# Attention score products of two neighbouring jobs on two row groups of TensorE, on unpadded keys

## The reference, cut to what matters

```
# second block: 8 heads, head size 64, two branches (slc, win) over 2 key groups, and 8 moba heads
s = q @ k.T * scale - slope * dist        # dist is huge where the key is masked
p = softmax(s);  out += gate * (p @ v)    # (moba: out = p @ v)
# third block, twice: 4 heads each of na, dil (head size 64), mla (96), diff (two halves of 32)
s = q @ k.T * scale + bias
p = softmax(s);  out = p @ v              # diff: out = (p0 - lam * p1) @ v
```

## Time and profile before

| | |
|---|---|
| median of 3 runs | 2133.78 us (2132.88 to 2137.18) |
| span of the profiled execution | 2125.6 us; no time of its own is listed for it, and the median of the runs stands 8.2 us above the span |
| busy share of the span | PE 80%, PE weight loads 58%, DVE 38%, ACT 30%, POOL 4% |
| woven attention stages | second block 1267 to 1389 us; third block 1490 to 1571 us and 1825 to 1907 us |
| granted clock in them | 1.00 of full speed, 0.83 and 0.90 in the last 15 us of each layer of the third block |

### The profile page before, as it was taken

The page is one execution under the profiler, slowest core; times in us unless marked ns, Lnnn a source line. Parts: engine busy times, 40 slices in busy tenths (PEclk is TensorE's granted clock), DMA queues, the critical chain, the costliest instruction groups (busy, mean ns, idle before and its releaser), DMA issues.

```text
span 2125.6 us, 32653 instructions
## 1 busy us (share of the span) xinstructions
PE 1698.7 (80%) x13430; PEld 1230.6 (58%) x13430; DVE 808.9 (38%) x1592; ACT 646.7 (30%) x1144; POOL 84.0 (4%) x143
## 2 busy tenths in 40 slices
PE   5999975656665665666665799988999999999998
PEld 3889921211111221111111599988989988989996
DVE  2374621001101111100111457775656654666654
ACT  3334310000000000000000347654754434655433
POOL 2000010000000000000000200101100001000000
PEclk9999988877878778777778799999999999999999
DMA  9986789999999999999999853408065545146650
GB/s 367 334 317 230 287 366 428 429 429 427 429 429 429 429 429 429 427 429 428 429 429 429 321 199 120 140 18 285 21 197 165 195 170 179 53 139 189 198 179 20
DMA packets 152994, 613.49 MB, mean 289 GB/s; under 512 B 8816, under 2 KB 62138, under 8 KB 128312
## 3 DMA queue, kind: packets, MB, share of 16 engines
q1 hardware_dynamic: 148928, 604.47, 72.4%
q0 software_dynamic: 3200, 7.14, 1.2%
q10 hardware_dynamic: 760, 0.39, 0.1%
HBM read 610.88 MB, written 5.03 MB: 290 GB/s over the span
## 4 chain that ended last, share of the span: by engine, by line
PE 54%; DMA 38%; DVE 3%; ACT 1%; issue 1%; SPq 1%; DVEq 1%; POOL 0%; POOLq 0%; ACTq 0%
PE psum L1473 52%; DMA ring<-in_w_down_e 19%; DMA ring<-in_w_up_e 18%; DMA ring<-in_w_in 1%; PE psum L1843 1%; DVE ring_r L704 1%; SPq L750 0%; ACT arena L1070 0%; ACT ring_r L695 0%; PE psum L1578 0%; SPq L769 0%; DVE arena L2448 0%; POOL stat L945 0%; PE psum L2007 0%; PE psum L1992 0%
## 5 line engine op out<-in xcount | busy, mean ns | idle before, releaser
L1473 PE MATMUL psum<-ring,arena 128*32 128x512 f32 (+2 forms) x4314 | 537.6, 643 | 279.9 <-DMA ring<-in_w_up_e 128.1
L1473 PE MATMUL psum<-xR_r,ring_r 128*128 128x256 f32 x4416 | 542.9, 281 | 2.1 <-DVE xR_r L2087 1.3
L1473 PEld LDWEIGHTS psum<-xR_r,ring_r 128*128 128x128 f32 x4416 | 521.0, 188 | 12.7 <-issue 10.8
L1473 PEld LDWEIGHTS psum<-ring,arena 128*32 128x32 f32 x4314 | 155.3, 134 | 629.8 <-issue 211.9
L704 DVE TENSOR_TENSOR ring_r<-ring,ring_r 128x1024 fp32r<-128x1024 f32 (+2 forms) x332 | 377.9, 1172 | 192.0 <-ACT ring_r L695 191.3
L695 ACT CAST ring_r<-ring 128x1024 fp32r<-128x1024 f32 (+2 forms) x332 | 320.3, 1007 | 382.1 <-PE psum L1473 377.9
L1473 PE MATMUL psum<-arena 128*128 128x256 f32 (+7 forms) x1270 | 188.0, 374 | 21.2 <-DVE arena L2323 9.9
L2320 DVE TENSOR_TENSOR arena<-arena,psum 128x512 f32<-128x512 f32 x16 | 16.9, 1055 | 476.8 <-PE psum L1473 476.8
L1473 PE MATMUL psum<-ring_r,xR_r 128*128 128x256 f32 (+3 forms) x1344 | 170.8, 284 | 10.5 <-DVE xR_r L2072 6.9
L1473 PE MATMUL psum<-ring_r,arena_r 128*128 128x512 f32 (+1 forms) x912 | 168.2, 346 | 2.1 <-DVE mt L2699 2.1
L1473 PEld LDWEIGHTS psum<-ring_r,xR_r 128*128 128x128 f32 x1344 | 160.6, 191 | 13.2 <-DVE ring_r L704 7.2
(11 more groups left out here) (270 smaller groups left out, 959.6 us busy)
## 6 DMA issues: line engine op xcount, KB each, us to landing
ring<-in_w_gate_e SPq DMA_DIRECT2D x64, 2048.0 KB, 25.9
ring<-in_w_down_e SPq DMA_DIRECT2D x63, 2048.0 KB, 26.4
ring<-in_w_up_e SPq DMA_DIRECT2D x62, 2048.0 KB, 24.9
ring<-in_w_in SPq DMA_DIRECT2D x30, 2048.0 KB, 12.5
ring<-in_w_ada SPq DMA_DIRECT2D x12, 2048.0 KB, 13.8
ring<-in_w_gate SPq DMA_DIRECT2D x22, 1024.0 KB, 5.5
ring<-in_w_up SPq DMA_DIRECT2D x22, 1024.0 KB, 8.2
ring<-in_w_down SPq DMA_DIRECT2D x10, 2048.0 KB, 7.8
```

The costliest lines, as they stand in the source:

```text
L1473: return nc.tensor.matmul(o, l, r, start=s, stop=e)
```

## The change

The score products lose their padding and are issued in pairs. Jobs are ordered so that jobs n and n+1 (n even) are the two heads of one partition pair with the same t (slc, win, moba, na, dil), or the two halves of one diff head. At the even slot PE issues both score products, the first into bank 4 from its own rows, the second into bank 5 from its own rows; at the odd slot it issues none. Before the pair PE waits until DVE has read both scores of the pair before. DVE runs `least` for both jobs at the even slot and for none at the odd one; everything else stays in its slot. `jmin`, `jsum` and `jrec` get eight columns instead of four. The keys are stored once (`ksD`, `kwD`, `kbT`, `knT`, `kdT`), so ACT takes them in one copy, and POOL's clearing of the padded keys goes. mla jobs (96 rows) are issued in pairs too, on the rows they had. The core of the diff:

```diff
-JOBS3 = ([("na", h, 0, t) for h in range(4) for t in range(TT)]
+JOBS3 = ([("na", 2 * m + f, 0, t) for m in range(2) for t in range(TT) for f in range(2)]
...
-NSA_JOBS = [(br, h, t) for h in range(8) for br in ("slc", "win") for t in range(TT)]
-MOBA_JOBS = [("moba", h, t) for h in range(8) for t in range(TT)]
+NSA_JOBS = [(br, 2 * m + f, t) for m in range(4) for br in ("slc", "win") for t in range(TT) for f in range(2)]
+MOBA_JOBS = [("moba", 2 * m + f, t) for m in range(4) for t in range(TT) for f in range(2)]
...
+            rows_ = slice(HD * (h % 2), HD * (h % 2) + HD)
+            if kind == "diff":
+                rows_ = slice(HD * (h % 2) + 32 * c, HD * (h % 2) + 32 * c + 32)
+            kp = (kdT if kind == "diff" else knT)[rows_, h // 2, :]
...
-            return dict(q=qaT[:, h // 2, qs], k=kk[:, h % 2, g, 0:nk], widths=[P] * (t + 1), dist=dist,
+            kk, vv, i = (ksD, vs, 1) if br == "slc" else (kwD, vw, 2)
+            return dict(q=qaT[rows_, h // 2, qs], k=kk[rows_, g, 0:nk], widths=[P] * (t + 1), dist=dist,
...
-                pool.wait_ge(n3_xn, l * 3 + 2)
-                if l == 0:
-                    nc.gpsimd.memset(arena[:, 2 * D:3 * D], 0.0).then_inc(pad3_set, 1)
-                nc.gpsimd.memset(kdP.rearrange("p m f c t -> p (m f c t)"), 0.0).then_inc(pad3_set, 1)
...
-                        for lo, rows, d in KP[n]:
-                            o = nc.scalar.copy(d[lo:lo + rows], two(G(i)[lo:lo + rows, :]))
-                        o.then_inc(g3_free[i % 4], 1)
+                    elif n in KN:
+                        take(n, KN[n], src=two, l=l)
...
-            def scores(j, J, s_, m_, base=0):
+            def scores(j, pair_, s_, m_, base=0):
                 if j >= 2:
-                    pe.wait_ge(m_, base + (j - 1))
-                mm(psum[:, 4 + j % 2, 0:sum(J["widths"])], J["q"], J["k"]).then_inc(s_, 1)
+                    pe.wait_ge(m_, base + j)
+                for f, J in enumerate(pair_):
+                    mm(psum[:, 4 + f, 0:sum(J["widths"])], J["q"], J["k"]).then_inc(s_, 1)
...
-                        scores(n, job3(n, l), k_s, k_min, l * NJ3)
+                        if n % 2 == 0:
+                            scores(n, (job3(n, l), job3(n + 1, l)), k_s, k_min, l * NJ3)
...
-                    least(n, job2(n), j_s, j_t, j_min, t_need=n - 3 if n >= 4 else None)
+                    for j in ((n, n + 1) if n % 2 == 0 else ()):
+                        least(j, job2(j), j_s, j_t, j_min, t_need=j - 3 if j >= 4 else None)
```

More of the change, by code:

```diff
@@ L160 @@
 assert len(L3) % RING == 0
[L163 removed]
+JOBS3 = ([("na", 2 * m + f, 0, t) for m in range(2) for t in range(TT) for f in range(2)]
          + [("mla", h, 0, t) for h in range(4) for t in range(TT)]
          + [("diff", h, c, t) for h in range(4) for t in range(TT) for c in range(2)]
[L166 removed]
+         + [("dil", 2 * m + f, 0, t) for m in range(2) for t in range(TT) for f in range(2)])
 NJ3 = len(JOBS3)
@@ L1330, in _ @@
                 elif n[:2] == "kb":
-                    i = AT[n]
-                    piece(act, i)
-                    for f in range(2):
-                        o = nc.scalar.copy(kbP[HD * f:HD * f + HD, 2 * h:2 * h + 2, f, :], two(G(i)[HD * f:HD * f + HD, :]))
-                    o.then_inc(g_free[i % 4], 1)
+                    take(n, kbT[:, 2 * h:2 * h + 2, :], src=two)
                 elif n[:2] == "vb":
@@ L2607, in _ @@
                             biases(l)
-                        turned = l * NT3 + (TURN3[n - 4] + 1) if n - 4 in TURN3 else None
-                        least(n, job3(n, l), k_s, k_t, k_min, l * NJ3, sbuf3, turned)
+                        for j in ((n, n + 1) if n % 2 == 0 else ()):
+                            turned = l * NT3 + (TURN3[j - 4] + 1) if j - 4 in TURN3 else None
+                            least(j, job3(j, l), k_s, k_t, k_min, l * NJ3, sbuf3, turned)
                         if n >= 1 and PAIR3[n - 1]:
```

68 lines of the change are left out of this document (30 added, 38 removed).

## The result

The changed kernel takes 2148.78 us (median of 4 runs, 2147.16 to 2150.91) against 2134.41 us of the kernel before, measured beside it: ratio 1.0072, 95% interval 1.0056 to 1.0088 (the two medians by themselves give 1.0067). It is slower by 14.4 us; 10.8 were forecast, and the time lies inside the forecast's own range (2139 to 2151). A second comparison, with 6 runs of the changed kernel, gave 1.0081 (1.0065 to 1.0097).

What follows compares the result with a forecast made beforehand. PE was taken to bound the woven attention stages. Terms 0.3 + 7.2 + 5.3 - 2.0 = +10.8 us on a 2125.6 us span, with the median 8.2 above, gave 2144.6 us; forecast range 2139 to 2151, 8-in-10 range 2131 to 2154.

Steps and rivals of the forecast that it cites:

- second `least` ahead of `both` and `finish`: Woven stages: DVE's second `least` delays what PE waits for, 7.2 us at diff turns and 5.3 us for `finish`.
- PE's own work, +0.3: Woven attention stages: 44 pairs of 256 keys at -0.04 us and 12 of 128 at +0.17, sum +0.3 us.
- the rival that row groups enter and leave for nothing: Score pairs on PE: entry and exit cost nothing, giving 2131 us; chance 0.2 for nothing or nearly (2127 to 2136).
- Waits at diff turns, +7.2: Third block: PE waits 0.60 us for `both` at six diff turns in each of two layers, +7.2 us.
- Waits for `finish`, +5.3: Second block, t = 1 pairs: 8 waits of 0.47 us, 3 smaller for moba, two late 128-key places; +5.3 us.
- Key copies, -2.0: ACT's four key copies become one: -0.9 us a layer in the third block, -0.2 in the second; -2.0 us.
- Tail, 0: Last four jobs of each layer: the same work of values and `finish` is only reordered, 0 us.
- The median stands 8.2 above it: Whole kernel: 8.2 us added to the predicted span of 2136.4 to get the median, 2144.6 us.
- What the profile was to show: Stages grow some 5 us (second block) and 3 a layer, PE's busy time falls, waits for `both` and `finish` appear.

Runs made afterwards that it cites:

- `both` between: Changed kernel with `both` and `finish` moved between the two `least` at the even slot; 2135.47 us against 2132.91 of the kernel before, ratio 1.0014.
- order and storage alone: Kernel before with only the new job order and unpadded keys in one copy, no pairs or row groups, full rows; 2134.8 us against 2133.38, ratio 0.9999.
- the runs without pairs: Changed kernel with each score product on its row group and `least` in its own slot: 2169.85 us, ratio 1.0163 to before; same with full rows: 0.9999.
- Putting `least` back: Changed kernel with each job's `least` in its own slot again, score pairs kept; 2140.77 us against 2133.38 of the kernel before, ratio 1.0036.

## Why the prediction was right, by its own steps

Three of the kernels above split the change into its steps, since each differs from the next in one of them (us, all three stages to the last product of probabilities and values):

| step | forecast | the two kernels | difference |
|---|---|---|---|
| second `least` ahead of `both` and `finish` | +12.5 | changed, less `both` between | +12.3 |
| pairs on row groups | +0.3 | `both` between, less order and storage alone | +1.1 |
| order of jobs and key storage | -2.0 | order and storage alone, less before | +0.5 |
| sum | +10.8 | changed, less before | +13.9 |

The large step was priced rightly, place by place; the two small ones came out 0.8 and 2.5 us dearer. (Two profiles of one kernel differ by 0.1 and 0.3 us in this sum; a part of the first row may be the clock, see the tail below.) That the exponentials add up to just the forecast 10.8 is chance: they leave out 3 us at the ends of the layers.

**PE's own work, +0.3: right.** The way in, the two rounds, the way out and the exposed weights all have their forecast size in the rows above: 0.63 us for the pair, 1.10 with the values (forecast 1.11). The prediction priced entry and exit of row groups by column groups, for want of a row; the runs without pairs confirm the choice at 0.29 us a visit, and the rival that row groups enter and leave for nothing (2131 us) is refuted by the same runs. They were forecast to cost 0.29 each too, but of other parts: the second record's weights are exposed also in a single product (0.63 for two records), and behind it only 0.05 are (1290.88 to 1291.04, 0.16 instead of 0.11). With the way in, 0.09, that makes 0.34, of which 0.29 reached the stage; that the forecast's figure came out is in part luck. A pair of 128 keys takes 0.42 us to the next full record (1279.35 to 1279.77) where two full products take 0.44, so with the way in and the weights behind it the pair costs, as forecast.

**Waits at diff turns, +7.2: right in place and number, nearly in size.** Six a layer were forecast and six are there. At the pair shown the wait is 0.62 us by starts, 0.60 forecast. By the waits' view, which counts from the end of the last record, the twelve add up to 2.9 + 3.1 = 6.0 us. Putting `both` between the two `least` gave 6.6 us back in the two layers, to the last product.

**Waits for `finish`, +5.3: right.** Eight waits at slc and win pairs with t = 1 were forecast. There are seven for L2440, one of 0.75 us and six of 0.36 to 0.38, and an eighth place where ScalarE's copy of the turned tile came last (0.38): 3.3 us, 0.42 each, for 0.40 forecast. Moba has 0.16 at two, the price forecast for three. Two late places at 128-key pairs behind two splits were counted with 0.4 each, and had 0.25 and 0.38. Putting `least` back gave 5.3 us in this stage, putting `finish` between the two 5.6.

**Key copies, -2.0: about right in the third block, wrong in the second.** The layers give 0.8 and 1.1 us (0.8 and 0.2 to the last product), and the 0.7 us wait for ScalarE behind the four copies is gone. The second block of the kernel with order and storage alone is 1.4 us longer where -0.2 stood; the order of the jobs, which I had not priced at all, is the likely cause.

**Tail, 0: too low.** The time from the last exponential of layer 2 to the next stage's products grew from 39.7 us (1903.6 to 1943.3) to 42.0 (1918.7 to 1960.7), and to 41.2 in the second profile; in layer 1 it is 40.6 before, and 41.9 and 40.8. A part of this is the end mark, since the last exponential comes earlier in the changed kernel. Another is the clock, which fell at the end of layer 2 in both kernels, but sooner in the changed one (second profile of before, then changed; columns as above):

```profile
1905.00:1908.00 3.00, 1.86 (x10) 1.56 (x10) 0.84 (x5) 0.37 (x1) 0.00 (x0) 0.71 1.10 348
1914.00:1917.00 3.00, 3.00 (x12) 1.91 (x12) 2.92 (x7) 1.07 (x5) 1.12 (x1) 0.50 1.06 388
```

In the kernel before this is the first stretch below 1.00, behind the last exponential (1903.6), and the clock is back at 1.00 after 7 us, in both profiles. In the changed kernel it fell 4.7 us ahead of the last exponential (1918.7) and stayed down for 17 us, in its second profile for 14. The kernel with `both` between has pairs too and 7 us, so this is not bound to them. The granted clock was 0.94 over the 60 us before that stage in the kernel before, and 0.86 and 0.89 in the two profiles of the changed one. Something similar stands at the change of layer, where the repeat of the kernel before shows

```profile
1784.00:1788.00 4.00, 1.49 (x7) 0.91 (x5) 3.06 (x5) 2.03 (x6) 1.25 (x3) 1.00 1.05 366
1788.00:1792.00 4.00, 3.45 (x30) 3.45 (x31) 1.22 (x5) 1.71 (x6) 2.57 (x3) 1.00 1.04 396
```

and the repeat of the changed kernel (same columns as above)

```profile
1796.00:1800.00 4.00, 1.43 (x9) 1.04 (x8) 2.03 (x6) 1.45 (x4) 1.79 (x5) 0.88 1.04 368
1800.00:1804.00 4.00, 3.89 (x18) 3.89 (x19) 1.85 (x6) 1.68 (x4) 0.00 (x0) 0.50 0.85 321
```

In both TensorE had stood still for some 2.5 of 4 us; in one the clock fell to its lower level (0.50, 1.2 GHz) and 18 products ran in 4 us where the other got through 30 in 3.45. From the start of the gate/up stage to the next layer's first exponential this makes 228.4 us against 226.0, with 119.0 us of gate/up in both. The first profile of the kernel before had a dip there too (0.88 and 0.69 in two stretches of 4 us), so it isn't the change's own. Whether the change makes it more frequent two profiles of each can't say. Between the two repeats' spans (2148.2 and 2132.6) lie 15.6 us: 14.2 in the stages to their last product, and 1.4 by which the second block's first exponential came later (1271.5 against 1270.1; over all 13 profiles it varies from 1269.8 to 1275.0). What stands between the layers (1.5 longer) and behind layer 2 (1.6 shorter) cancels. How much of the layers' growth is the clock and not the waits stays open.

**"The median stands 8.2 above the span": a wrong reading that did no harm.** Each run's time is its span plus 1.8 to 1.9 us, with few exceptions. The rest was the pace of the gate/up stages: the one profiled execution of before had the fast pace twice, 2 x 4.5 = 9 us that most of the timed runs, to go by their times, did not have in full. Adding the distance to the median was right for the median, but the spans of the two first profiles differ by 23.4 us, and the change made only about 15 of them.

**What the profile was to show.** The prediction names some 5 us for the second block and some 3 for each layer, though its own terms add up to 6.7 and 2.1. Measured to the last product it is 6.8 and 6.9, and 2.7 to 4.4. "PE's busy time falls" was wrong: between the first and the last exponential it rose from 113.9 to 117.1 us in the second block, and was 68.5 and 70.0 us in the layers where it had been 68.5. Busy is the union of records, and these get longer at each way in and out and at the lower clock.

## What to carry to other kernels

Two products that run side by side on row groups save one product's time, and each visit to the groups costs 0.3 to 0.4 us in a dense stream of full products, however many stand in it: by these prices a pair of 256 columns about breaks even and one of 128 loses, and four products in one visit gained (8 us over pairs in the runs here). When a producer delivers two results at once, the consumer need not take both at once: what another engine waits for goes between them. And a reordering that leaves the sum of work unchanged has to be costed at the instruction for which the busiest engine waits next, from both sides, since that engine also arrives sooner. And a stage is to be measured between instructions whose place in the stream the change leaves alone: the exponentials hid 3 of 14 us here, and showed 9.6 us of gain where the time had 6.6.

## What the runs showed of the hardware that was not expected

- The pace of a dense stream of 1008 products of 128x256 has two values at one and the same granted clock of 1.00, 114.5 / 1008 = 0.1136 and 119.0 / 1008 = 0.1181 us a product, kept through the whole stage. It differs between executions and between layers of one execution, and is worth up to 9 us here, more than half of what the change costs. Why is open.
- Two single-product records on a row group take 0.63 us until the next full product, exactly as four on two groups do.
- At the change of layer a stretch of 4 us in which TensorE is busy for 1.2 to 1.9 us is followed by the lower clock in some executions and not in others. In one execution a single wait of 1.13 us, with 1.78 of 3 us busy ahead of it, was followed by it too (0.69).
